# Strassen's seven products for the FFN up projections, from the fifth row pair of each layer on

## The reference, cut to what matters

```python
def conv_ffn(x, w_up, w_conv, b_conv, w_down):
    h = causal_dwconv(x @ w_up, w_conv, b_conv)      # 3 taps along the tokens
    gate, val = jnp.split(h, 2, axis=-1)
    return (jax.nn.silu(gate) * val) @ w_down

# in second_block, for layer 0 and 1:
h = h + conv_ffn(rmsnorm(h, ffn_norm_g[layer]), ffn_w_up[layer], ffn_conv_w[layer],
                 ffn_conv_b[layer], ffn_w_down[layer])
```

## Time and profile before

| | us |
|---|---|
| median of 3 runs | 1993.69 |
| lowest, highest | 1991.33, 1995.39 |
| profiled execution, its span from first to last instruction | 1994.6 |
| PE busy in it | 1904.1 (95%) |
| DVE busy | 1078.8 (54%) |
| ACT busy | 894.8 (45%) |
| POOL busy | 660.5 (33%) |

### The profile page before, as it was taken

The page is one execution under the profiler, slowest core; times in us unless marked ns, Lnnn a source line. Parts: engine busy times, 40 slices in busy tenths (PEclk is TensorE's granted clock), DMA queues, the critical chain, the costliest instruction groups (busy, mean ns, idle before and its releaser), DMA issues.

```text
span 1994.6 us, 29273 instructions
## 1 busy us (share of the span) xinstructions
PE 1904.1 (95%) x11647; PEld 1572.4 (79%) x11647; DVE 1078.8 (54%) x1511; ACT 894.8 (45%) x1239; POOL 660.5 (33%) x286
## 2 busy tenths in 40 slices
PE   5999999998989999989899999999999999999997
PEld 4888888886877888778657888888888788888886
DVE  5223777775267656858985551354535655513544
ACT  4444777776246445463334441344322344423432
POOL 1323232234211111143314444443444434444433
PEclk8999999998999999999999999999999999999999
DMA  8221112123111111132202323223323223232321
GB/s 304 69 69 48 57 57 104 54 74 140 53 60 54 45 53 54 54 105 65 84 22 85 106 88 103 95 95 96 95 95 95 85 84 106 87 104 95 95 96 53
DMA packets 48823, 168.71 MB, mean 85 GB/s; under 512 B 5552, under 2 KB 7856, under 8 KB 48688
## 3 DMA queue, kind: packets, MB, share of 16 engines
q1 hardware_dynamic: 46384, 162.03, 24.8%
q10 hardware_dynamic: 2304, 4.81, 0.7%
HBM read 164.72 MB, written 2.10 MB: 84 GB/s over the span
## 4 chain that ended last, share of the span: by engine, by line
PE 59%; DVE 8%; ACT 2%; issue 1%; DMA 0%; POOL 0%; ACTq 0%; DVEq 0%
PE ps L575 19%; PE ps L576 18%; PE ps L577 18%; DVE wS L2162 1%; DVE X L1640 1%; DVE wS L1634 1%; ACT sq L1112 1%; PE ps L892 1%; DVE tab_tmp L1634 1%; PE ps L825 0%; DVE sp L1634 0%; DVE tmp L1634 0%; DVE acc L1634 0%; DVE tmp L1640 0%; DVE hf L1634 0%
## 5 line engine op out<-in xcount | busy, mean ns | idle before, releaser
L1618 POOL TENSOR_TENSOR wlo<-raw,whi 128x1024 fp32r<-128x1024 f32 x241 | 586.5, 2446 | 1096.5 <-ACT whi L1094 1096.5
L1094 ACT ACTIVATE whi<-raw 128x1024 fp32r<-128x1024 f32 x251 | 258.5, 1056 | 506.0 <-PE ps L577 495.6
L575 PE MATMUL ps<-Ahi,whi 128*128 128x512 f32 (+1 forms) x784 | 309.4, 395 | 12.4 <-POOL wlo L1618 5.2
L577 PE MATMUL ps<-Ahi,wlo 128*128 128x512 f32 (+1 forms) x784 | 305.6, 390 | 0.0
L576 PE MATMUL ps<-Alo,whi 128*128 128x512 f32 (+1 forms) x784 | 304.3, 388 | 0.0
L575 PEld LDWEIGHTS ps<-Ahi,whi 128*128 128x128 f32 x784 | 148.5, 189 | 47.2 <-issue 7.1
L1634 DVE TENSOR_TENSOR ps<-ps,rstd 128x1024 f32<-128x1024 f32 (+1 forms) x60 | 69.7, 1161 | 210.4 <-PE ps L577 179.2
L576 PEld LDWEIGHTS ps<-Alo,whi 128*128 128x128 f32 x784 | 148.4, 189 | 31.7 <-issue 0.5
L577 PEld LDWEIGHTS ps<-Ahi,wlo 128*128 128x128 f32 x784 | 148.3, 189 | 31.8
L1640 DVE SCALAR_TENSOR_TENSOR cv<-ps,vec,cv 128x511 f32<-128x511 f32 (+1 forms) x176 | 131.9, 749 | 70.6 <-ACT cv L1112 66.0
L575 PE MATMUL ps<-Fhi,whi 128*128 128x512 f32 (+1 forms) x427 | 166.5, 390 | 2.8 <-DVE Flo L1634 2.8
(11 more groups left out here) (296 smaller groups left out, 3884.7 us busy)
## 6 DMA issues: line engine op xcount, KB each, us to landing
raw<-in_units SPq DMA_DIRECT2D x299, 512.0 KB, 3.6
X<-in_xT SPq DMA_DIRECT2D x4, 512.0 KB, 9.6
X<-in_xT ACTq DMA_DIRECT2D x4, 512.0 KB, 5.1
out_xT<-X SPq DMA_DIRECT2D x8, 256.0 KB, 2.3
CX<-in_ctxT SPq DMA_DIRECT2D x4, 256.0 KB, 9.7
acc<-in_rope ACTq DMA_DIRECT2D x1, 384.0 KB, 3.1
gmw<-in_gmw ACTq DMA_DIRECT2D x1, 384.0 KB, 3.5
bs<-in_bs ACTq DMA_DIRECT2D x1, 384.0 KB, 4.2
```

Source lines behind the costliest of these rows:

```text
L575: nc.tensor.matmul(out, sh, mh, start=first, stop=False)
L577: return nc.tensor.matmul(out, sl, mh, start=False, stop=last)
L1094: nc.scalar.activation(whi[:, s % CONV, :], raw[:, c % RAW, :], ACT.Copy).then_inc(sem("whi"), 1)
L1618: nc.gpsimd.tensor_tensor(wlo[:, s % CONV, :], raw[:, plan.unit_at[("split", s)] % RAW, :], whi[:, s % CONV, :].bitcast(fp32), ALU.subtrac ...
```

## The change

The first four rows of each layer (PLAIN = 4) stay as they are. The other 36 rows (`SEVENS`: 7 in the first half and 11 in the second half of each layer) are made by Strassen's scheme in the Winograd form. The product of a row is seen as a 2x2 block product: the weights are cut into gate and val, and into inner tiles 0 to 3 and 4 to 7; the activations are cut into the same inner halves and into token halves of 256. Seven block products take the place of eight. A block product is four inner tiles times three products with 256 moving columns.

The seven forms of the activations (three plain blocks, four sums T1 to T4) are made once per layer during the four plain rows: DVE's `forms` and `forms_low`, ACT's `forms_high`, one POOL subtraction for each of the four inner tiles. The norm is now in them, so a Strassen row has no `scaled`. The sums of weight blocks are made for every row: `sum_13` (128x1024), `sum_2` and `sum_4` (128x512 each) on DVE. A row now has the weight parts A and B from two loaded units, C (1024 wide) and E (512 wide) from sums, and all four are split by ACT and POOL. The seven products land in two PSUM tiles (`ua`, `ub`) and are combined by `first_sum`, `middle_sums` and `last_sum` on DVE and by two copies on ACT into `C2` in SBUF, from which the taps are taken. DVE handles in one turn the taps and the gate of row u-1, the weight sums of row u+1 and the output sums of row u. Buffers moved to make room: Bhi/Blo now serve both layers, Mhi/Mlo and Phi/Plo take over in the short convolution between them.

The diff, cut to its core:

```diff
+PLAIN = 4
+HT, HK = T // 2, KD // 2
+X11, X21, X22, T1, T3, T2, T4 = range(7)
+SEVENS = [(l, f, j) for l in range(2) for f in range(2) for j in range(FH) if f or j >= PLAIN]
...
+FORMS_AT = [[0], [1, 2], [3], []]
...
+            def seven(u):
+                l, f, j = SEVENS[u]
+                y, x = opened(("ub", u), True), opened(("ua", u), True)
+                r6, r3, r7 = (y[:, i * HT:(i + 1) * HT] for i in range(3))
+                r1, r4, r5 = (x[:, i * HT:(i + 1) * HT] for i in (0, 2, 3))
+                def multiply(part, half, form, r, onto=False):
+                    s = plan.pair_of[part, u]
+                    lows(s)
+                    for k in range(HK):
+                        if SEVENS[u][1:] == (0, PLAIN):
+                            pe.wait_ge(sem("zlo" if form in (X11, X21, X22) else "ztl"), HK * l + k + 1)
+                        c = slice((HK * half + k) * P, (HK * half + k + 1) * P)
+                        stat = (w4hi[:, c], w4lo[:, c]) if part == "E" else (whi[:, plan.ring[s], c], wlo[:, plan.ring[s], c])
+                        last = product(r, stat, (Zhi[:, form, k, :], Zlo[:, form, k, :]), k == 0 and not onto, k == HK - 1, onto)
+                    return last
+                multiply("A", 0, X11, r1).then_inc(sem("f1"), 1)
+                multiply("A", 1, T4, r4).then_inc(sem("fa"), 1)
+                multiply("E", 0, T2, r6).then_inc(sem("fv"), 1)
+                multiply("C", 0, T3, r7)
+                multiply("C", 1, T1, r5).then_inc(sem("fq"), 1)
+                pe.wait_ge(sem("fV"), u + 1)
+                done(multiply("B", 0, X22, r3), ("ub", u))
+                pe.wait_ge(sem("c1"), u + 1)
+                done(multiply("B", 1, X21, r1, True), ("ua", u))
...
+            def forms_high(l, k):
+                y, z = C2[:, k % 2, :, :], HK * l + k
+                ac.wait_ge(sem("zy"), 2 * z + 2)
+                act(Zhi[:, X11, k, :], y[:, 0, 0:HT], ACT.Copy, sem_name="zh")
+                act(Zhi[:, X21:X22 + 1, k, :], y[:, 1, :].rearrange("p (i t) -> p i t", i=2), ACT.Copy, sem_name="zh")
+                ac.wait_ge(sem("zt"), 3 * z + 3)
+                act(Zhi[:, T1:T4 + 1, k, :], Tf[k % 2], ACT.Copy, sem_name="zth")
+                forms_at.append((converted[0], l, k))
...
+            def val_part(u):
+                l, f, r = SEVENS[u]
+                j, c = (2 * l + f) * FH + r, (2 + f) * FH + r
+                ac.wait_ge(sem("c2"), u + 1)
+                if j >= 3:
+                    ac.wait_ge(sem("hf"), hf_of(j - 3))
+                act(cv[:, j % 3, 1, :], C2[:, u % 2, 1, :], ACT.Identity, v_(f"ffn_b{l}", c), v_(f"ffn_w{l}", 88 + c), "ca")
+            def gate_part(u):
+                l, f, r = SEVENS[u]
+                j, c, n = (2 * l + f) * FH + r, f * FH + r, plan.index[("ua", u)]
+                ac.wait_ge(sem("psum"), n + 1)
+                act(C2[:, u % 2, 0, 0:HT], PS[plan.slot[n]][:, 0:HT], ACT.Copy, sem_name="c11")
+                ac.wait_ge(sem("c12"), u + 1)
+                act(cv[:, j % 3, 0, :], C2[:, u % 2, 0, :], ACT.Identity, v_(f"ffn_b{l}", c), v_(f"ffn_w{l}", 88 + c), "ca")
+            def first_part(u):
+                n = plan.index["ua", u]
+                ac.wait_ge(sem("f1"), u + 1)
+                if u:
+                    ac.wait_ge(sem("fV"), u)
+                act(held_r1, PS[plan.slot[n]][:, 0:HT], ACT.Copy, sem_name="c1")
+            def silu(u):
+                l, f, r = SEVENS[u]
+                j = (2 * l + f) * FH + r
+                ac.wait_ge(sem("conv"), 4 * j + 4)
+                act(tmp[:, j % 2, 0:T], cv[:, j % 3, 0, :], ACT.Silu, sem_name="se")
...
+                    for r in range(0 if f else PLAIN, FH + 1):
+                        before, now, after = ((l, f, r + i) in SEVENS for i in (-1, 0, 1))
+                        u = SEVENS.index((l, f, r - 1)) + 1 if before else SEVENS.index((l, f, r))
+                        ends = plan.pair_of["B", u if now else u - 1]
+                        if before:
+                            gate_part(u - 1)
+                        up_to(ends if now else ends + 3)
+                        if now:
+                            first_part(u)
+                            up_to(ends + 1)
+                        if before:
+                            silu(u - 1)
+                            high(Fhi[:, r - 1, :])
+                        if now:
+                            up_to(ends + 3 if after else ends + 2)
+                            val_part(u)
...
+                while forms_at and forms_at[0][0] <= s:
+                    _, l, k = forms_at.pop(0)
+                    po.wait_ge(sem("zth"), HK * l + k + 1)
+                    nc.gpsimd.tensor_tensor(Zlo[:, T1:T4 + 1, k, :], Tf[k % 2], Zhi[:, T1:T4 + 1, k, :].bitcast(fp32),
+                                            ALU.subtract).then_inc(sem("ztl"), 1)
...
+                    if part == "E":
+                        nc.gpsimd.tensor_tensor(w4lo[:, :], sum2[:, :], w4hi[:, :].bitcast(fp32),
+                                                ALU.subtract).then_inc(sem("wlo"), 1)
...
+            def forms(l, k):
+                y, t, z = C2[:, k % 2, :, :], Tf[k % 2], HK * l + k
+                if z > 1:
+                    need(("zh", 2 * z - 2), ("ztl", z - 1))
+                made = [mark(STTi(y[:, i, :], X[:, k + HK * i, :], v_(f"ffn_g{l}", k + HK * i), rstd[:, 0:T], MUL, MUL), "zy")
+                        for i in range(2)]
+                need(*made)
+                x12 = y[:, 0, HT:T].rearrange("p (o t) -> p o t", o=1).to_broadcast([P, 2, HT])
+                x11 = y[:, 0, 0:HT]
+                x11_22 = bass.AP(x11.tensor, x11.offset, [x11.ap[0], [T + HT, 2], [1, HT]])
+                need(mark(TTi(t[:, 0:2, :], x12, x11_22, SUB), "zt"))
+                need(mark(TTi(t[:, 2, :], y[:, 1, HT:T], t[:, 0, :], SUB), "zt"))
+                need(mark(TTi(t[:, 3, :], y[:, 1, 0:HT], t[:, 2, :], SUB), "zt"))
+            def forms_low(l, k):
+                y = C2[:, k % 2, :, :]
+                need(("zh", 2 * (HK * l + k) + 2))
+                two = y[:, 1, :].rearrange("p (i t) -> p i t", i=2)
+                tt(Zlo[:, X11, k, :], y[:, 0, 0:HT], Zhi[:, X11, k, :].bitcast(fp32), SUB)
+                tt(Zlo[:, X21:X22 + 1, k, :], two, Zhi[:, X21:X22 + 1, k, :].bitcast(fp32), SUB, "zlo")
+            def raw_of(part, u):
+                c = plan.unit_at[("split", plan.pair_of[part, u])]
+                need((f"ld{c % RAW}", 16 * (c // RAW + 1)))
+                return raw[:, c % RAW, :]
+            def sum_13(u):
+                a, b = raw_of("A", u), raw_of("B", u)
+                if u:
+                    need(plan.low_sem[plan.pair_of["C", u - 1]])
+                w21 = b[:, 0:T].rearrange("p (o t) -> p o t", o=1).to_broadcast([P, 2, T])
+                mark(TTi(sum13.rearrange("p (o t) -> p o t", o=2), w21, a.rearrange("p (o t) -> p o t", o=2), ADD), "s13")
+            def sum_2(u):
+                if u:
+                    need(plan.low_sem[plan.pair_of["E", u - 1]])
+                need(("s13", u + 1))
+                mark(TTi(sum2[:, :], sum13[:, 0:T], raw_of("A", u)[:, T:2 * T], ADD), "s2")
+            def sum_4(u):
+                need(("s2", u + 1))
+                b = raw_of("B", u)
+                mark(TTi(b[:, 0:T], sum2[:, :], b[:, T:2 * T], ADD), "s4")
+            def regions(u):
+                y, x = (PS[plan.slot[plan.index[key, u]]] for key in ("ub", "ua"))
+                return x, y
+            def first_sum(u):
+                _, y = regions(u)
+                need(("fv", u + 1), ("c1", u + 1))
+                mark(TTi(vacc, y[:, 0:HT], held_r1, SUB), "fV")
+            def middle_sums(u):
+                x, y = regions(u)
+                need(("fq", u + 1), ("fV", u + 1))
+                q = mark(TTi(qacc, vacc, y[:, T:T + HT], ADD), "fQ")
+                mark(TTi(wacc, vacc, x[:, T + HT:2 * T], ADD), "fW")
+                need(q)
+                both = qacc.rearrange("p (o t) -> p o t", o=1).to_broadcast([P, 2, HT])
+                mark(TTi(C2[:, u % 2, 1, :].rearrange("p (i t) -> p i t", i=2), both,
+                         x[:, T:2 * T].rearrange("p (i t) -> p i t", i=2), ADD), "c2")
+            def last_sum(u):
+                _, y = regions(u)
+                need(("psum", plan.index["ub", u] + 1), ("fW", u + 1))
+                mark(TTi(C2[:, u % 2, 0, HT:T], y[:, HT:T], wacc, SUB), "c12")
+            def taps(u):
+                l, f, r = SEVENS[u]
+                j = (2 * l + f) * FH + r
+                need(("ca", 2 * j + 2), ("c12", u + 1))
+                for n, (back, part) in enumerate([(1, 1), (1, 0), (2, 1), (2, 0)]):
+                    if n > 1:
+                        need(("conv", 4 * j + n - 1))
+                    c = (part * 2 + f) * FH + r
+                    y = cv[:, j % 3, part, back:T]
```

(38 more changed lines are left out.)

230 lines of the change are left out of this document (165 added, 65 removed).

## The result

| | us |
|---|---|
| changed kernel, median of 4 runs (lowest to highest) | 2190.03 (2189.57 to 2195.75) |
| kernel before, 4 runs beside it | 1994.54 (1991.33 to 1998.63) |
| ratio, 95% interval | 1.0976, 1.0947 to 1.1005 |
| profiled execution of the changed kernel, its span | 2194.0 |

A forecast was written before the change was run, and what follows sets the result against it. PE bounded the old kernel; in the new rows, POOL subtractions and DVE operations with two SBUF operands would exclude each other. 2 x (59 + 41) = +200 us on 1994.6, stated as 2194 us; 8-in-10 range 2115 to 2280.

The forecast's parts named there:

- PE row 11.03 to 9.54: PE in a Strassen row: 84 products of 256 columns at 0.1136 us take 9.54 us, 1.49 less than 11.03.
- DVE 9.4 alone: DVE's instructions of one Strassen row, undisturbed, sum to 9.4 us, where it was 5.6.
- POOL 8.5 alone: POOL's four subtractions of one Strassen row, undisturbed, sum to 8.5 us, where it was 4.8.
- Exclusion, row 15.5: Strassen rows: POOL subtractions and DVE operations with two SBUF operands exclude each other, so a row takes 15.5 us.
- The floor of 14.4: Strassen row: 7.0 us on DVE plus 8.5 on POOL, 1.1 off for handovers, if the shared path never idles.
- the layout in order of time: One Strassen row's instructions placed in time on all engines; next taps and next B begin near 15.7 us.
- Opening, +59 a layer: First half of a layer, plain rows, forms and first Strassen rows: ends at 1250.1 instead of 1191.2, +59 us (+40 to +75).
- Second half, +41 a layer: Second half of a layer, Strassen rows without backlog at the start: 162.0 us instead of 120.9, +41 us.
- Sum +200: Whole kernel, both halves of both layers: 2 x (59 + 41) = +200 us.
- Rival: the clock falls too: PE waits each Strassen row and drops to half clock, slowing the last two products; 2264 us; chance 0.15.
- the engines hide each other's work: Strassen rows: every engine stays below 9.54 us, a row under 11.03, total 1947 us; chance 0.04.
- partial exclusion: Strassen rows: path shared only in part, or some operations cheaper; rows 12 to 13.5 us, about 2090; chance 0.08.

The follow-up runs named there:

- e1: Changed kernel with POOL's subtractions narrowed to 16 columns in every Strassen row but the very first, leaving out work; 1997.5 us, 1.0011 of before.
- e2: Changed kernel with POOL's subtraction replaced by three memsets of the same place in every Strassen row but the very first; 2021.7 us, 1.0133 of before.
- e3: Changed kernel with the combined row left in PSUM, where the taps read it, and ACT's copy of block 11 dropped; complete; 2105.3 us, 1.055 of before.
- e5: e3 plus silu output and `hf` written into PSUM tile `ua`, and `Flo` moved ahead of `middle_sums`; complete; 2120.3 us, 1.0614 of before.
- e6: e1 plus narrowed low parts for the plain rows' units and a memset for the low parts of T1 to T4; 1981.9 us, 0.9917 of before.
- e4: Changed kernel with 24 further useless products of 256 columns on PE in each row, between E and C; 2183.2 us, 1.0947 of before.
- e8: e5 with `last_sum` moved ahead of `sum_4` in DVE's queue, nothing else; 2089.1 us, 1.0474 of before.

## Why the prediction was right, point by point

- **PE row 11.03 to 9.54.** 9.60 in e1, where PE is the bound. Right: 0.1143 us a product.
- **DVE 9.4 alone.** 8.35. The sum of own lengths was right for each instruction (746, 680, 1218, 412), but in a dense queue the next begins about 0.07 to 0.09 us before the last ends (1314.20 for 0.42, then 1314.54, in e1), over 13 joints some 1 us. End to end e1's instructions are 9.46 us a row, and they occupy 8.35.
- **POOL 8.5 alone.** 9.5 us of busy time a row, including what DVE blocks (means 2728 and 2845 for 2.41). `w4lo` took 1.286 where 1.28 was estimated.
- **Exclusion, row 15.5.** 15.36, shown from both sides: it goes when POOL's reads go (e1), stays away when POOL only writes (e2), goes tap by tap with the operand in PSUM (e3, e5). But the sum by which I bounded it, DVE's excluded 7.0 plus POOL's 8.5, hit 15.5 by luck. In the eight rows a POOL subtraction or a DVE operation with two SBUF operands is running for 14.15 us a row, 1.35 less than the sum, since neighbouring instructions and handovers overlap, and the path is idle for 1.2; the two nearly cancel. The floor of 14.4 was set too high: DVE's excluded instructions occupy 6.6 us in e1, not 7.0, which makes it 14.0. And the sum says nothing of the idle time: by it e5 should have had rows near 10.6, and with 3.2 us idle it had 13.7. POOL is not always in turn either: it waits 5.9 us a row for ACT's high parts (46.8 in eight rows). DVE's occupied time, 8.35 of its own and 6.8 of blocking, accounts for the row but is measured, not forecast; only the layout in order of time forecasts it. It gave 15.7, again with two errors that nearly cancel: 1.0 us too much up to `first_sum`, 0.5 too little behind it.
- **Opening, +59 a layer.** The up rows of the first half took 176.8 and 177.2 us instead of 121.7: +55. The first `first_sum` came 80.9 us after the first up product, 86.0 were laid out (1069.47 to 1155.5). The mis-sized term is the blocking, 14 us and 2.4 for a POOL turn in the fourth row: e6 shows 9.4. The rest of the queue took some 2 us more than laid out. That the weights of plain rows 3 and 4 would be late, but not later than the forms, held: PE waits 4.85 and 7.04 us for them, 6.65 for the first Strassen weights and 2.27 for a `Zlo` of DVE, and `first_sum` comes out of DVE's queue, straight behind `sum_13` (1148.55 to 1149.77). But PE has hardly any slack there: at half clock from 1133.3 to 1147.0, it has waited only 0.23 us when `first_sum` releases it. What the half clock costs an opening was not tried by itself; in e4 both openings are 1.6 to 1.8 us shorter.
- **Second half, +41 a layer.** 164.6 and 165.0 instead of 120.8: +44. The second `first_sum` came 22.8 us after the start (21 said). The opening's error of -4 us a layer and this one of +3 offset each other; that the total is within 4 us of 2194 is in part luck.
- **Sum +200.** 683.6 - 485.1 = +198.5 in the up stages of the profiled execution, which took 5.7 us more than the median; the down products kept full pace (264 steps in 60.6 us from 1245.58 to 1306.18, 0.2295 each).
- **Rival: the clock falls too.** The clock did fall; it cost next to nothing. In these rows it is at half level behind each wait of PE, alternately for 6.8 and for 3.4 us, and the last two products of a row take 5.4 or 4.6 us, where they take 3.1 at full clock (in most rows of e8). Rows with 5.4 last 15.38 to 15.41 us, rows with 4.6 last 15.31 or 15.32: 0.8 us of PE costs the row 0.08. In one of the longer kind:

```profile
1359.68:1363.10 3.42, 2.95 (x14) 2.96 (x15) 3.39 (x8) 2.20 (x4) 0.86 (x1) 0.50 0.17 43
1363.10:1366.50 3.40, 3.40 (x22) 3.40 (x22) 3.40 (x3) 1.50 (x4) 3.22 (x2) 0.66 0.29 111
```

The products start at 1360.15, 0.21 us apart (1.2 GHz), and PE is done at 1365.6. ACT then has the gate half ready at 1366.93; `Flo`, blocked by POOL, ends at 1366.87, and the taps begin at 1367.01. So nearly all of the half clock is hidden behind `Flo`, more than the 1.3 of 2.7 us that I had allowed, and e4, which lifts the mean clock, gains 7 us in all.
- **Rivals: the engines hide each other's work; partial exclusion.** Refuted by the groups above.

The best complete version was e8, 4.7% over before. What remains for it is a DVE queue of 8.35 us with three sums that read two SBUF operands, and a first half that takes 35 us more a layer than the old one (156.8 and 157.0 against 121.7). No complete version beat the kernel before.

## What to carry to other kernels

Before moving work from PE to the vector engines, list each DVE instruction by where its operands lie. Those with two SBUF operands pay a POOL subtraction's remaining time whenever they meet one, and so does everything queued behind them; so lay the row out in order of time: adding up the shared path gives how long it is in use, not how long it stands idle. An operand left in PSUM frees its reader, but the next blocked instruction takes its place, and a blocked one belongs behind what another engine waits for. A saving in the steady rows must also pay for the stage that prepares them: e1 had 51 us less work for PE (36 x 1.43) and ended level with before.

## What the runs showed of the hardware

- POOL's memset of 128x1024 takes 955 ns and leaves a DVE operation with SBUF operands at its own length (746 ns), while POOL's subtraction of the same size (2.41 us) stretches the same taps to a mean of 1812. I had not expected the kind of POOL instruction to decide it so cleanly.
- Operations of DVE with one PSUM operand kept 742, 682 and 677 ns beside POOL at full work, also where PSUM was the output as well.
- Blocking works both ways and does not go by size. In e1 a 128x16 subtraction on POOL takes 0.22 us when DVE is elsewhere, and DVE's means (746, 680) show nothing of it; but the ones for B and A come while DVE works on SBUF operands and take 0.41 us behind a tap and 1.42 behind `sum_13`:

```profile
L1818 POOL TENSOR_TENSOR wlo<-raw,whi 128x16 fp32r<-128x16 f32 x15 | 14.2, 946 | 30.4 <-ACT whi L1203 30.4
```

- In the changed kernel (steady rows of layer 0's second half) the granted clock was 0.5 for 6.8 us about each PE wait of 3.6 to 5.2 us and for 3.4 us about each of 2.9 to 3.0, and 1.0 between. In e8, with a wait of 2.2 us in every row, it was 0.5 for 3.4 us in every third row alone.
